# Mamba/MoE block and hybrid attention block in one kernel: the pass between them and q, k, v in another order

## The reference, cut to what matters

```python
# end of the first block
x = x + g2 * moe_ffn(h2, ...)             # per token: sum over 4 picks of weight * expert row, and biases
x = x * rsqrt(mean(x * x) + EPS) * final_norm_w
# start of the second
h = concatenate([meta, x])                # 528 tokens
xn = h * rsqrt(mean(h * h) + EPS) * norm1_g
q, k, v, xr, gr, g_merge = split(xn @ w_in)
q, k = rope(rms(q) * q_norm_g), rope(rms(k) * k_norm_g)
attn = softmax(q @ k.T * HEAD_DIM ** -0.5) @ v
```

## Time and profile before

| | |
|---|---|
| median of 3 runs | 3396.39 us (3394.14 to 3403.73) |
| the profiled execution | 3396.01 us |
| its span (first to last instruction) | 3394.2 us |
| TensorE / VectorE / ScalarE / GpSimd busy | 3220.5 (95%) / 1314.4 (39%) / 728.1 (21%) / 421.9 (12%) us |
| mean granted TensorE clock | 0.981 of 2.4 GHz |

### The profile page before, as it was taken

How to read it: one execution, slowest core, us unless ns; L and a number is a source line. 1 busy time by engine, 2 the same in 40 slices (tenths; PEclk the granted TensorE clock), 3 DMA queues, 4 the chain that set the end, 5 groups by cost and what they waited for, 6 DMA issues and landing times.

```text
span 3394.2 us, 40465 instructions
## 1 busy us (share of the span) xinstructions
PE 3220.5 (95%) x13878; PEld 1904.8 (56%) x13879; DVE 1314.4 (39%) x2077; ACT 728.1 (21%) x1300; POOL 421.9 (12%) x329
## 2 busy tenths in 40 slices
PE   7999999999999999999999999998989999999999
PEld 5555555556488833333333333332767888788887
DVE  2545444464434521221221221221455477443342
ACT  3212121211021111111111111111314355211100
POOL 0212222232100100000000000000312254000000
PEclk9999999999999999999999999999899999999999
DMA  4212111124612479999999997796330121222211
GB/s 199 71 60 67 63 63 67 59 106 154 223 50 79 171 258 383 391 393 380 380 393 389 393 377 288 301 378 253 120 133 8 41 84 47 84 73 78 73 75 53
DMA packets 185077, 615.68 MB, mean 181 GB/s; under 512 B 18176, under 2 KB 55168, under 8 KB 174240
## 3 DMA queue, kind: packets, MB, share of 16 engines
q1 hardware_dynamic: 161216, 552.79, 42.6%
q0 software_dynamic: 10944, 39.85, 3.3%
q10 hardware_dynamic: 12832, 21.88, 1.8%
HBM read 578.01 MB, written 36.44 MB: 181 GB/s over the span
## 4 chain that ended last, share of the span: by engine, by line
PE 80%; DMA 6%; issue 5%; DVE 4%; ACT 2%; POOL 2%; SPq 1%; ACTq 0%; DVEq 0%; POOLq 0%
PE ps L312 23%; PE ps L2208 16%; PE ps L2182 10%; PE ps L1890 6%; PE ps L261 6%; DMA slot<-in_w_exp 5%; PE ps L1959 3%; PE ps L2416 2%; PE ps L1969 2%; PE ps L1935 1%; PE ps L2388 1%; PE ps L1974 1%; PE ps L1827 1%; PE ps L2371 1%; PE ps L2177 1%
## 5 line engine op out<-in xcount | busy, mean ns | idle before, releaser
L2208 PE MATMUL ps<-slot,xT_blk 128*64 128x512 f32 x3200 | 735.1, 600 | 29.6 <-DMA slot<-in_w_exp 27.4
L2208 PEld LDWEIGHTS ps<-slot,xT_blk 128*64 128x64 f32 x3200 | 218.3, 137 | 467.5 <-issue 377.1
L2182 PE MATMUL ps<-slot,aT 128*64 128x512 f32 x1632 | 362.8, 597 | 0.9 <-ACT aT L1619 0.9
L1890 PE MATMUL ps<-hT,slot 128*128 128x512 f32 (+1 forms) x896 | 309.1, 503 | 1.1 <-ACT small L1416 1.1
L2182 PEld LDWEIGHTS ps<-slot,aT 128*64 128x64 f32 x1632 | 117.4, 137 | 237.9 <-issue 237.9
L1890 PEld LDWEIGHTS ps<-hT,slot 128*128 128x128 f32 x896 | 169.2, 191 | 130.1 <-issue 121.2
L2915 DVE TENSOR_TENSOR gate<-ps,b_row 128x512 f32<-128x512 f32 x50 | 34.6, 692 | 521.0 <-PE ps L2208 521.0
L2536 DVE SCALAR_TENSOR_TENSOR conv<-ps,g_conv,conv 128x510 f32<-128x510 f32 (+1 forms) x224 | 133.3, 631 | 198.2 <-ACT conv L1429 194.8
L2911 DVE MEMSET b_there<- 128x1 f32 x50 | 3.0, 59 | 385.9 <-DMA b_few<-in_b_gu 377.1
L312 PE MATMUL ps<-in_t,in_s 128*128 128x264 f32 x528 | 124.8, 386 | 0.5 <-issue 0.5
L3267 POOL TENSOR_TENSOR token_there<-cst 128x1 f32<-128x1 f32 x25 | 4.8, 194 | 952.5 <-PE ps L2173 952.5
(11 more groups left out here) (499 smaller groups left out, 4789.1 us busy)
## 6 DMA issues: line engine op xcount, KB each, us to landing
slot<-in_w_exp SPq DMA_DIRECT2D x768, 512.0 KB, 8.6
in_w<-in_w_ffn SPq DMA_DIRECT2D x22, 1024.0 KB, 4.8
expert_rows<-zero SPq DMA_DIRECT2D x4, 4608.0 KB, 22.5
slot<-in_w_xbc SPq DMA_DIRECT2D x8, 2048.0 KB, 9.8
w_modT<-in_w_modT POOLq DMA_DIRECT2D x32, 512.0 KB, 3.6
rnn_w<-in_w_rnn SPq DMA_DIRECT2D x16, 1024.0 KB, 4.8
expert_rows<-y_row ACTq DMA_DIRECT2D x102, 128.0 KB, 5.5
out_w<-in_w_ffn_out SPq DMA_DIRECT2D x8, 1408.0 KB, 7.5
```

The lines of the kernel that those rows point to most:

```text
L1890: last = pe.matmul(ps[:, 2 * (m % 2) + part, 0:n], w[:, (k * 4 + m % 4) * P:(k * 4 + m % 4 + 1) * P], hT[:, k, c0:c0 + n], start=(k == 0), ...
L2182: last = pe.matmul(ps[h * UNIT:(h + 1) * UNIT, 6, :], aT[:, t, d * UNIT:(d + 1) * UNIT], slot[4 + d][:, t * D + h * 512:t * D + (h + 1) * ...
L2208: last = pe.matmul(ps[h * UNIT:(h + 1) * UNIT, 2 * s + t, :], xT_blk[:, k, s * UNIT:(s + 1) * UNIT], slot[i // 4][:, at:at + 512], start=( ...
```

## The change

- ScalarE copies `weightT` before it waits for the last rows' store. TensorE runs `keep_warm` of 19 products, not 14, ahead of the meta tokens' sum, not behind it.
- The picks of a tile are gathered in the order 0, 3, 1, 2; a semaphore counts the first three, another the last. Same number of gathers.
- The order of the tiles' steps changes on every engine (below); ScalarE no longer weighs tile 3, and VectorE does weighing and scaling of it in eight steps, of which TensorE's first q tile waits for one at a time; tile 2 is scaled by VectorE, not GpSimd. `keep_warm(6, 0)` ahead of the last sum goes.
- q's tiles are written out without a loop on TensorE. The last q tile's rotary products go behind the first tile of the next round or of k/v, k's behind k1 and v0. `sum_x` goes into the middle of v1, into bank 4.
- Scores 0 come before v's transposes, v's copies behind exp 0 on ScalarE; an exp on one column stands in front.
- The first block's norm leaves GpSimd: VectorE inverts a quarter of the columns in each of the steps 3 to 6 of the attention and makes one weighted step in each of the steps 8 to 15. GpSimd's four sums of `xnT` wait for `times3` to `times6`, its `sums(0)` for `times17` and for VectorE's norm.

The lists of step names are changed to match and left out here.

```diff
...
+def one(self, pe, j, it, ready=None):
+    i, m = divmod(j, self.tiles)
+    if m == 0:
+        pe.wait_ge(self.loaded[self.slots[i]], it * 16 + (self.first[i] + 16))
+    if j >= 2:
+        self.ev.after(pe, f"tile{j - 2}", it)
+    else:
+        self.ev.after_last(pe, f"tile{j - 2 + self.n}", it)
+    self.tile(pe, self.slots[i], m, j, ready)
...
+    self.sum_x3(dve, x)
+    self.sum_x4(dve, x)
+def sum_x3(self, dve, x):
...
+def sum_x4(self, dve, x):
...
+back_pe.after(act, "weightT")
+back_act.done(act.activation(weightT[:], ps[0:NE, 4, 0:TT * P].rearrange("p (t c) -> p t c", c=P), ACT.Copy), "weightT")
...
-back_pe.after(act, "weightT")
-back_act.done(act.activation(weightT[:], ps[0:NE, 4, 0:TT * P].rearrange("p (t c) -> p t c", c=P), ACT.Copy), "weightT")
...
-back_pe.after(act, "meta")
-back_act.done(act.activation(inverse_meta[:], ps[:, 6, 0:N_META], ACT.Sqrt, scale=1.0 / D, bias=eps_col), "meta_root")
...
-    act.wait_ge(s_rows[t % 2][0], 32 * (t // 2 + 1))
+    act.wait_ge(s_rows[t % 2][0], 48 * (t // 2 + 1))
...
-first_pick(0)
-first_pick(1)
-for t in range(TT):
+def squared(t):
...
+def weighed(t):
...
-    if t + 2 < TT:
-        first_pick(t + 2)
+def rooted(t):
...
+first_pick(0)
+back_pe.after(act, "meta")
+back_act.done(act.activation(inverse_meta[:], ps[:, 6, 0:N_META], ACT.Sqrt, scale=1.0 / D, bias=eps_col), "meta_root")
+first_pick(1)
+first_pick(2)
+squared(0)
+weighed(0)
+rooted(0)
+first_pick(3)
+squared(1)
+weighed(1)
+squared(2)
+weighed(2)
+squared(3)
+rooted(1)
+rooted(2)
+rooted(3)
...
+kv_in.ev.open(act)
...
+k_rot.act.open(act)
...
+last_round = q_in.rounds - 1
+for j in range(NKV):
+    q_rot.pe.after(act, f"turn{2 + j}", last_round)
+    q_rot.dve.after(act, f"out{2 + j}", last_round)
+    k_rot.on_act(act, j, 0)
+kv_in.pe.after(act, f"tile{NKV}")
+kv_in.ev.done(act.activation(vT[0][:], ps[:, 0:2, 0:H2], ACT.Copy), f"tile{NKV}")
...
-back_act.done(act.activation(inverse_x[:], ps[:, 7, :], ACT.Sqrt, scale=1.0 / D, bias=eps_col), "root_x")
-kv_in.ev.open(act)
-k_rot.act.open(act)
-q_rot.dve.all(act)
-for j in range(NKV):
-    k_rot.on_act(act, j, 0)
-for j in range(NKV):
-    kv_in.pe.after(act, f"tile{NKV + j}")
-    kv_in.ev.done(act.activation(vT[j][:], ps[:, 2 * j:2 * j + 2, 0:H2], ACT.Copy), f"tile{NKV + j}")
-for j in range(NKV):
+back_act.done(act.activation(inverse_x[:], ps[:, 4, :], ACT.Sqrt, scale=1.0 / D, bias=eps_col), "root_x")
+kv_in.pe.after(act, f"tile{NKV + 1}")
+kv_in.ev.done(act.activation(vT[1][:], ps[:, 2:4, 0:H2], ACT.Copy), f"tile{NKV + 1}")
+act.activation(square_h[0][:, 0, 0:1], eps_col, ACT.Exp)
+def v_rows(j):
...
-v_act.all(act)
-k_rot.dve.all(act)
...
+    if g == 0:
+        for j in range(NKV):
+            v_rows(j)
...
+table_dve.all(pe)
+keep_warm(19, 7)
...
-table_dve.all(pe)
-keep_warm(14, 7)
...
-    pe.wait_ge(s_rows[t % 2][1], 32 * (t // 2 + 1))
+    pe.wait_ge(s_rows[t % 2][0], 48 * (t // 2 + 1))
...
-for t in range(1, TT):
-    turn_sum(t)
-    sum_squares(t - 1)
-keep_warm(6, 0)
-sum_squares(TT - 1)
+turn_sum(1)
+sum_squares(0)
+turn_sum(2)
+turn_sum(3)
+sum_squares(1)
+sum_squares(2)
+sum_squares(3)
...
-    back_dve.after(pe, "scaled")
-    back_pool.after(pe, f"scaled{TT - 2}")
+    back_dve.after(pe, f"scaled3_{k}")
+    if k == 0:
+        back_pool.after(pe, "scaled1")
...
-def q_besides(j, it):
-    if j >= 1:
-        q_rot.on_pe(pe, j - 1, it)
-    if j == q_in.n - 1:
-        q_rot.on_pe(pe, j, it)
-q_in.multiply(pe, q_besides, ready=normed)
+k_rot.pe.open(pe)
+for it in range(q_in.rounds):
+    for j in range(q_in.n):
+        q_in.one(pe, j, it, normed if it == j == 0 else None)
+        if j:
+            q_rot.on_pe(pe, j - 1, it)
+        elif it:
+            q_rot.on_pe(pe, q_in.n - 1, it - 1)
+last_round = q_in.rounds - 1
+def x_sum(k):
+    if k == KD // 2:
+        k_rot.act.after(pe, f"root{NKV - 1}")
+        back_pool.after(pe, f"acc{KD - 1}")
+        back_pe.done(pe.matmul(ps[:, 4, :], ones, acc_x[:], start=True, stop=True), "sum_x")
+q_in.ev.after(pe, f"tile{q_in.n - 2}", last_round)
+kv_in.one(pe, 0, 0)
+q_rot.on_pe(pe, q_in.n - 1, last_round)
...
-k_rot.pe.open(pe)
+kv_in.one(pe, 1, 0)
+q_rot.act.all(pe)
+q_rot.dve.after(pe, f"sin{q_in.n - 1}", last_round)
+k_rot.on_pe(pe, 0, 0)
+kv_in.one(pe, 2, 0)
+k_rot.on_pe(pe, 1, 0)
+kv_in.one(pe, 3, 0, x_sum)
...
-back_pool.after(pe, f"acc{KD - 1}")
-back_pe.done(pe.matmul(ps[:, 7, :], ones, acc_x[:], start=True, stop=True), "sum_x")
-def kv_besides(j, it):
-    if j == 1:
-        back_act.all(pe)
-    if 1 <= j <= NKV:
-        k_rot.on_pe(pe, j - 1, it)
-    if j == kv_in.n - 1:
-        k_rot.act.all(pe)
-        k_rot.dve.all(pe)
-        kv_in.ev.all(pe)
-        for v in range(NKV):
-            for k, (k0, nk) in enumerate(KEY_TILES):
-                last = pe.transpose(ps[0:nk, 4 + 2 * v + k // 4, (k % 4) * P:(k % 4 + 1) * P],
-                                    vT[v][:].rearrange("p a c -> p (a c)")[:, k0:k0 + nk], ident)
-            v_pe.done(last, f"turned{v}")
-kv_in.multiply(pe, kv_besides)
...
-v_act.all(pe)
+def turn_v(v):
+    if v == 0:
+        back_act.after(pe, "root_x")
+    kv_in.ev.after(pe, f"tile{NKV + v}")
+    for k, (k0, nk) in enumerate(KEY_TILES):
+        last = pe.transpose(ps[0:nk, 4 + 2 * v + k // 4, (k % 4) * P:(k % 4 + 1) * P],
+                            vT[v][:].rearrange("p a c -> p (a c)")[:, k0:k0 + nk], ident)
+    v_pe.done(last, f"turned{v}")
...
+        else:
+            kv_in.ev.after(pe, f"tile{NKV + g}")
...
+        if g == 0:
+            for v in range(NKV):
+                turn_v(v)
...
+        else:
+            v_act.all(pe)
...
-    dve.wait_ge(s_rows[t % 2][1], 32 * (t // 2 + 1))
+    dve.wait_ge(s_rows[t % 2][1], 16 * (t // 2 + 1))
...
-for t in range(TT):
-    add_picks(t)
-    if t:
-        add_back(t - 1)
-    if t > 1:
-        invert(t - 2)
-add_back(TT - 1)
-invert(TT - 2)
-invert(TT - 1)
-back_dve.after(dve, f"inverse{TT - 1}")
-last_tokens = xnT[:, :, token_part(TT - 1)]
-back_dve.done(dve.tensor_tensor(last_tokens, last_tokens,
-                                inverse_n[:, (TT - 1) * P:].unsqueeze(1).broadcast_to([P, KD, P]), ALU.mult), "scaled")
+add_picks(0)
+add_back(0)
+add_picks(1)
+add_picks(2)
+add_back(1)
+invert(0)
+add_picks(3)
+add_back(2)
+add_back(3)
+invert(1)
+invert(2)
+back_act.after(dve, "times2")
+back_dve.after(dve, "inverse2")
+third = xnT[:, :, token_part(2)]
+back_dve.done(dve.tensor_tensor(third, third, inverse_n[:, 2 * P:3 * P].unsqueeze(1).broadcast_to([P, KD, P]), ALU.mult), "scaled2")
+invert(3)
+back_dve.after(dve, "inverse3")
+for k in range(KD):
+    back_dve.done(dve.scalar_tensor_tensor(out=xnT[:, k, token_part(3)], in0=h2nd[:, k, token_part(3)], scalar=both_norms[:, k:k + 1],
+                                           in1=inverse_n[:, 3 * P:], op0=ALU.mult, op1=ALU.mult), f"scaled3_{k}")
...
+k_rot.dve.open(dve)
...
-back_act.after(dve, "root_x")
-back_dve.done(dve.reciprocal(inverse_x[:], inverse_x[:]), "inverse_x")
-k_rot.dve.open(dve)
...
-v_pe.all(dve)
...
+    if 3 <= g < 7:
+        x_quarter = inverse_x[:, (g - 3) * P:(g - 2) * P]
+        if g == 3:
+            back_act.after(dve, "root_x")
+        back_dve.done(dve.reciprocal(x_quarter, x_quarter), f"inverse_x{g - 3}")
+    if 8 <= g < 8 + KD:
+        k = g - 8
+        x_rows = h2nd[:, k, N_META:T2]
+        if k == 0:
+            back_dve.after(dve, "inverse_x3")
+        back_dve.done(dve.scalar_tensor_tensor(out=x_rows, in0=x_rows, scalar=prm[:, PRM["final"].start + k:PRM["final"].start + k + 1],
+                                               in1=inverse_x[:], op0=ALU.mult, op1=ALU.mult), f"normed{k}")
...
-        for h in range(2):
-            pool.wait_ge(s_rows[t % 2][h], 32 * (t // 2))
+        pool.wait_ge(s_rows[t % 2][0], 48 * (t // 2))
+        pool.wait_ge(s_rows[t % 2][1], 16 * (t // 2))
...
-    for k in range(TOPK):
+    for k in (0, 3, 1, 2):
...
-                                ).then_inc(s_rows[t % 2][k // 2], 16)
-for t in range(TT - 1):
+                                ).then_inc(s_rows[t % 2][int(k == 2)], 16)
+for t in range(2):
...
-back_dve.after(pool, "inverse_x")
-for k in range(KD):
-    x = h2nd[:, k, N_META:T2]
-    back_pool.done(pool.tensor_tensor(x, x, prm[:, PRM["final"].start + k:PRM["final"].start + k + 1].broadcast_to([P, SEQ]), ALU.mult),
-                   f"weighed{k}")
-    back_pool.after(pool, f"weighed{k}")
-    back_pool.done(pool.tensor_tensor(x, x, inverse_x[:], ALU.mult), f"normed{k}")
...
-rnn.sum_x(pool, xn_half)
+attn_dve.after(pool, "times3")
+rnn.sum_x1(pool, xn_half)
+attn_dve.after(pool, "times4")
+rnn.sum_x2(pool, xn_half)
+attn_dve.after(pool, "times5")
+rnn.sum_x3(pool, xn_half)
+attn_dve.after(pool, "times6")
+rnn.sum_x4(pool, xn_half)
...
+back_dve.all(pool)
+attn_dve.after(pool, "times17")
...
```

(13 more changed lines are left out.)

8 lines of the change are left out of this document (added).

## The result

The changed kernel takes 3365.10 us (median of four runs, 3360.08 to 3370.02) against 3395.62 of the kernel before: a ratio of 0.9902, 95% interval 0.9885 to 0.9920. Faster by 30.5 us, where 31.8 were forecast. A second comparison, run with the last experiments, gave 3366.73 against 3398.71, again 0.9902 (0.9885 to 0.9919), 32.0 us.

What follows compares the result with a forecast made beforehand. TensorE, busy 95% of the span, was taken as the bound, so only its waits and low-clock stretches could give time: 8.5 + 17.1 + 6.7 - 0.5 = 31.8 us off 3396.0, forecast 3364, range 3353 to 3375.

Steps and rivals of the forecast that it cites:

- B: Rival, before q: low clock from first bias product, scaled3 steps alternating, clock falling twice in the chain; 3370 us, chance 0.20.
- part 1: Stretch before q: earlier table copy, warming and new tile order, less clock falls and alternation; gain 8.5 us.
- (a): Before q: weight table's copy no longer waits for the store; bias products start at 2369.9, not 2376.66: 6.8 us.
- (b): Bias products before q: clock falls at 2372.6, three of eight at 0.9 us, five at 1.75, end at 2381.4.
- (c): Before q: keep_warm, 38 instructions instead of 28, goes ahead of the meta sum and takes 11.1 us; meta sum ends 2394.3.
- (e): From tile 0 turned to q: new order of the tiles' steps, first scaled3 at 25.9 us instead of 31.4, 5.5 less.
- (f): Costs in the chain to q: clock falling in TensorE's idle gaps, 1.5 us, and scaled3 steps beside GpSimd's sums, 2.
- The alternation of the scaled steps: Chain to q: VectorE's eight scaled3 steps taking turns with seven GpSimd sums; nothing to 4.1 us, taken as 2.
- Part 2: q, k, v: no tile waits for VectorE; q's start to last v tile's end 104.3 us, not 121.4; gain 17.1.
- Part 3: Attention: third turning sooner after the last v tile, where it took 15.7 us; gain 6.7, less 0.5 for added VectorE work.
- The norm's price: Attention: quarter reciprocals and weighted steps added to VectorE mostly fit its idle time; cost 0.5 us.
- D: Rival: TensorE's clock falls at the attention's start and isn't given back; slower than before, 3440 us, chance 0.01.

Runs made afterwards that it cites:

- the second profile: The changed kernel run again, unchanged, beside the last experiments: 3366.73 us (3363.52 to 3367.65), ratio 0.9902 to the kernel before.
- the experiment: Changed kernel with GpSimd's sums of squares waiting for VectorE's last scaled3 step: eight steps take 2.19 us, not 8.70; q's second tile 2.5 us earlier.

## Why the prediction was right, point by point

**Total.** 3364 against 3365.10; 31.8 us forecast, 30.5 measured, 32.0 in the second comparison. No rival came about; of B, two of the three parts did in some measure. The sign was never near: copy, round ends and attention start each show the wait that they removed. The total is nearer than its parts: part 1 came 3.2 short, the rest 0.9 over, and 1.0 of the 30.5 lies behind the attention, where nothing was changed. That the sum met the median within 1.1 us is in part luck.

**(a) The copy** gained 6.74 for 6.8, and the copy undone gives it back (7.1 at the bias products' start, 9.9 from M to q's second tile).

**(b), (c) The bias products and the warming.** 12.57 for 11.5, since the clock fell after two products and not three (0.73 over the first 3.6 us, so 1.7 of them at 1.00); then 9.77 for 11.1. The errors are of opposite sign, and M comes at 26.63 for 26.97. Runs of the same program had 11.88 and 10.62: where it falls is not known to a product, and the sum of the two moves less than either.

**(e), (f) The chain to q.** The gain of this step did not show. The new order of the tiles was put at 5.5 us less, against 3.5 for (f); from turned 0 to q's second tile it took 45.74 us before and 46.00 after, 44.27 in the second profile. Two sizes were off. The clock fell in front of tile 0's and tile 1's turning as allowed for, and cost 1.3 (3.08 for 1.80) and about 1.2 up to tile 3's pick, where 1.5 was taken in all. In the second profile it did not fall there, and part 1 gained 7.86 of the 8.5: so 2.6 of this profile's 3.2 is where the clock happened to fall. And a term was missing: `scaled0` on GpSimd beside tile 3's pick, 2.2 us. The working put (e)'s `scaled2` behind GpSimd's scaling of tile 1 (it measured 2.60) by the very row that shows this, but did not ask what GpSimd's other scaling stands beside. The alternation of the scaled steps, bounded between 0 and 4.1 and taken at 2, cost 2.5 by the experiment (the bound has a slip: a step each 1.5 where TensorE takes 0.89 makes 4.3); and it shows the sign that the prediction gave for it, a first q tile over 8 us. Together: 2.2 + 1.0 + 0.5 = 3.7, less 0.3 from M, is 3.4 short; measured 8.5 - 5.3 = 3.2.

**Part 2** gained 17.07 for 17.1, and no tile waits. The reasoning, 8.9 us of TensorE a tile against 6.9 of VectorE, holds, and the lower clock behind a wait was rightly counted in: undoing it costs 18.4, with 1.7 of it for a clock that fell at the first round's end in that run and not in the kernel before. That 17.07 met 17.1 so closely hangs on where it fell.

**Part 3** gained 7.11 for 6.7. By the experiments v's turnings behind scores 0 are worth 0.9, GpSimd's waits 2.0 and the exp ahead nothing. The rest, some 4.2, was not taken apart by a run. The chain of the kernel before has two pieces of it, the table load of 1.28 shown above and two instructions of TensorE at the lower clock:

```profile
2569.64 1.31 PE ps L2361 x5
2570.95 1.77 PE ps L2350 x4
```

The same two take 0.76 and 0.91 in the changed kernel, 1.4 less. The last 1.5, the shorter row of waits, is argued, not shown. That the table load ran beside the maxima was right, but it was not the added exp that did it.

**The norm's price** in the attention was 0.0 and not 0.5: the gap of 0.41 in front of the max was shortened, to 0.29 or to nothing where a norm step stood ahead of it. Where it was nothing the max did come later, 2.47 us behind the one before instead of 2.31, but the pair of steps still took 5.42, so the push was made up, as the working had it for the weighted steps.

**D** had no hold: the clock stood at 1.00 from q's second tile on (89.6 us without a gap) through the attention.

## What to carry to other kernels

Ask of each GpSimd instruction of some us which VectorE instruction it will stand beside, on both sides of a change: three times here VectorE steps on the critical path stood behind GpSimd, and a wait on GpSimd, which nobody missed, gave 2.0 to 2.5 us back each time. A software pipeline across round ends is worth the waits plus the clock that falls in them; here the waits could be sized beforehand from one engine's time per tile, and where the clock falls could not. Steps on an engine with idle time in every period can be free, as twelve of 0.7 to 0.95 us were here. Where the clock falls in one profile and not in the next, compare stretches of the same kind, or single instructions.

## What was not expected of the hardware

- TensorE busy 20.00 of 20.00 us, warming products of 256 columns and bias products of 32 rows in turn, stood at a granted clock of 0.50, and came back to 1.00 with the warming products alone, inside the next 4 us.
- The same program waited 2.23 and 2.36 us in front of two turnings in one profile, and they took 3.08 and 3.58 us; in another it waited 2.23 and 2.98, and the clock did not fall.
- Short VectorE steps and GpSimd instructions in line at the same time go one and one, each pair 1.35 us, where the VectorE steps by themselves take 0.27 (2.19 by eight).
- ScalarE's table load of 1.28 us started before what its exp waits for in one kernel, and behind it in another.
- The same program differs between executions by up to 9 us in the experts (the last rows' copy at 2361.84 and 2370.71) and by 2.6 in the stretch before q, by the instant at which the clock falls. The runs of the changed kernel lie between 3360 and 3370.
